# Routing and gathering from the unnormalised residual stream, with identity matmuls inside the first expert blocks, in a one-core encoder layer

## What is computed

```python
def rms_norm(x, g):
    y = x * lax.rsqrt(jnp.mean(x * x, axis=-1, keepdims=True) + EPS)
    return y * g

# h is the residual stream after cross attention; t = rms_norm(h, norm_ffn_g)
logits = jnp.dot(t, w_router) + b_router
top_v, top_i = lax.top_k(logits, TOP_K)
gates = jax.nn.softmax(top_v, axis=-1)
# for each expert e, for the tokens xb routed to it
hid = xb @ w_e1[e] + b_e1[e]
gate = jnp.minimum(hid[:, :D_FF], 7.0)
lin = jnp.clip(hid[:, D_FF:], -7.0, 7.0)
act = gate * jax.nn.sigmoid(1.702 * gate) * (lin + 1.0)
y = act @ w_e2[e] + b_e2[e]
# h + sum over the token's experts of gate weight * y, then rms_norm(., norm_final_g)
```

## Time and profile before

| | us |
|---|---|
| median of 3 runs (lowest, highest) | 1327.13 (1324.11, 1329.89) |
| the profiled execution | 1328.03 |
| its span, first to last instruction | 1326.1 |
| PE busy in the span | 1261.2 (95%) |
| DVE / ACT / POOL busy | 366.1 / 208.2 / 112.9 |
| PE waiting for weight chunks (L875: ring 15.0, stage 6.6, low 5.0) | 26.6 |
| moved by DMA | 456.83 MB, mean 344 GB/s |

### The profile page before, as it was taken

The page is one execution under the profiler, slowest core; times in us unless marked ns, Lnnn a source line. Parts: engine busy times, 40 slices in busy tenths (PEclk is TensorE's granted clock), DMA queues, the critical chain, the costliest instruction groups (busy, mean ns, idle before and its releaser), DMA issues.

```text
span 1326.1 us, 15280 instructions
## 1 busy us (share of the span) xinstructions
PE 1261.2 (95%) x6167; PEld 570.1 (43%) x6167; DVE 366.1 (28%) x785; ACT 208.2 (16%) x323; POOL 112.9 (9%) x109
## 2 busy tenths in 40 slices
PE   8999899999889999999999999999999999999996
PEld 3478785868643333333333333333333323333332
DVE  6478582021123111221112111122111111221112
ACT  2031422100311111111111111111111111111111
POOL 4599200010010000000000000000000000000000
PEclk9999899999999999999999999999999999999999
DMA  8533653449845999999999999999999999999995
GB/s 244 169 127 128 141 98 128 159 133 381 322 180 242 410 427 428 427 428 428 427 427 428 429 429 428 428 427 429 429 429 428 427 428 429 428 428 428 428 427 212
DMA packets 55128, 456.83 MB, mean 344 GB/s; under 512 B 4760, under 2 KB 6880, under 8 KB 30512
## 3 DMA queue, kind: packets, MB, share of 16 engines
q1 hardware_dynamic: 51744, 449.74, 82.3%
q0 software_dynamic: 2192, 5.99, 2.8%
q10 hardware_dynamic: 1152, 0.52, 0.2%
HBM read 454.11 MB, written 1.61 MB: 344 GB/s over the span
## 4 chain that ended last, share of the span: by engine, by line
PE 62%; DMA 29%; DVE 5%; ACT 3%; issue 1%; SPq 0%; ACTq 0%; DVEq 0%
PE pt L875 17%; DMA ring<-in_w_e 16%; PE pt L915 12%; DMA stage<-in_w_e 6%; DMA low<-in_w_e 6%; PE pt L476 6%; PE pt L489 6%; PE pt L524 4%; PE pt L456 3%; PE pt L842 3%; PE pt L829 3%; PE pt L537 2%; PE pt L881 1%; ACT wi_ L953 1%; DMA stage<-in_w_in 1%
## 5 line engine op out<-in xcount | busy, mean ns | idle before, releaser
L875 PE MATMUL pt<-ring,hres 128*64 128x512 f32 x1216 | 273.1, 595 | 15.3 <-DMA ring<-in_w_e 15.0
L875 PEld LDWEIGHTS pt<-ring,hres 128*64 128x64 f32 x1216 | 84.0, 137 | 198.7 <-issue 167.0
L915 PE MATMUL pt<-ring,wi_ 128*64 128x512 f32 x640 | 141.7, 595 | 5.4 <-ACT wi_ L953 5.4
L1560 DVE TENSOR_SCALAR hnt<-pt 128x512 f32<-128x512 f32 x32 | 22.1, 692 | 308.1 <-PE pt L875 308.1
L1506 DVE COPY ct_<-ct_ 128x2 f32 (+1 forms) x33 | 5.6, 170 | 363.7 <-PE pt L875 359.2
L875 PE MATMUL pt<-stage,hres 128*64 128x512 f32 x416 | 93.9, 595 | 6.6 <-DMA stage<-in_w_e 6.6
L875 PE MATMUL pt<-low,hres 128*64 128x512 f32 x416 | 93.8, 595 | 5.0 <-DMA low<-in_w_e 5.0
L1122 ACT ACTIVATE hnt<-hnt 128x512 f32<-128x512 f32 x32 | 20.2, 630 | 477.9 <-DVE hnt L1560 477.9
L915 PEld LDWEIGHTS pt<-ring,wi_ 128*64 128x64 f32 x640 | 44.5, 137 | 89.7 <-issue 82.4
L842 PE MATMUL pt<-big,lamb 64*128 64x512 f32 x256 | 63.6, 615 | 0.7 <-ACT big L953 0.7
L829 PE MATMUL pt<-a,ct_ 128*64 128x512 f32 x264 | 62.3, 593 | 0.0
(11 more groups left out here) (312 smaller groups left out, 1272.2 us busy)
## 6 DMA issues: line engine op xcount, KB each, us to landing
ring<-in_w_e SPq DMA_DIRECT2D x116, 2048.0 KB, 40.2
low<-in_w_e SPq DMA_DIRECT2D x38, 2048.0 KB, 41.0
stage<-in_w_e SPq DMA_DIRECT2D x38, 2048.0 KB, 40.1
stage<-in_w_in SPq DMA_DIRECT2D x16, 1024.0 KB, 6.7
stage<-in_w_xkv SPq DMA_DIRECT2D x8, 1024.0 KB, 5.9
stage<-in_w_mix_out SPq DMA_DIRECT2D x4, 1024.0 KB, 4.9
stage<-in_w_xq SPq DMA_DIRECT2D x4, 1024.0 KB, 4.9
stage<-in_w_xo SPq DMA_DIRECT2D x4, 1024.0 KB, 16.2
```

The lines of the kernel that those rows point to most:

```text
L875: last = pe.matmul(pt[PC][SLOTS * g:SLOTS * (g + 1), 512 * b:512 * (b + 1)], xT[:, k % 4, k // 4], ring_slot[n][:, c:c + 512], start=(k == ...
L915: last = pe.matmul(pt[PD][SLOTS * h:SLOTS * (h + 1), 512:1024], hT[:, c, g], ring_slot[n][:, D * c + 512 * h:D * c + 512 * (h + 1)], start ...
L1560: dve.tensor_scalar(hg, pt[PC][:, 0:512], GATE_MAX, None, ALU.min).then_inc(m_g2, 1)
```

## The change

- The router no longer reads normalised tokens. PE transposes the raw residual stream, in strided pieces (`by_k`), inside the second tile of `xo`: eight transposes for tile 0 after 4 matmuls, four for the first half of tile 1 after 12, the last four after `route(0)`. The second tile's residual sum is made in two halves.
- The gain is folded on POOL into the router weights, once, long before. The norm factor `r3` multiplies the logits (inside the bias addition) and the selection matrix `sel`. The gather reads `h3`, and the gain is applied in the product that replaces the copy to `xT` (`block_tokens`). `normed`, `gained_tile` and POOL's two products for this norm go away, and so does the load of the broadcast gain.
- The rank of expert 0 is used directly for its selection; positions, negated maxima, softmax of the gates, table of extra blocks and transposed gates come later, partly between the w_e1 chunks of the first block (`first_block_between`). The first gather is in two halves with copies on ACT and DVE.
- The identity matmuls: tile 0's two are around the rank matmuls, tile 1's go into blocks 0 and 1, `add_bias` into block 2. The bias matmuls of a block move from its first to its second w_e1 chunk.
- In every block ACT takes the sigmoid from PSUM without waiting for DVE's clamp, and the elementwise chain has three DVE operations where it had four.

The diff, cut to its core and with eight blanks of indentation taken off:

```diff
...
+xgn = a2[:, 0:512]
+xT_flat = a2[:, 512:1024]
 xT = xT_flat.rearrange("p (c n s) -> p c n s", c=4, n=2)
-hg, hl, hgl, hsg = (hnt[:, 512 * i:512 * (i + 1)] for i in range(4))
+hl, hsg, ysb = (hnt[:, 512 * i:512 * (i + 1)] for i in range(3))
+h0T = hnT[:, :, 0:P]
+h1T = a2[:, 0:KD * P].rearrange("p (k l) -> p k l", k=KD)
+by_k = [h3[:, t].rearrange("p (j q r) -> p j r q", j=W1_CHUNKS, r=2) for t in range(NT)]
+ffn_gain = gains[:, 3 * KD:4 * KD]
...
-    pool.dma_start(gffn, T["norm_ffn_g"].broadcast_to([P, D])).then_inc(s_gf, 16)
...
-    pool.wait_ge(s_gf, 16)
-    pool.wait_ge(S["tokp"], 8)
...
-        pool.tensor_tensor(xk, xk, gk, ALU.mult).then_inc(S["hn3"], 1)
+    pool.wait_ge(s_rt, 112)
+    pool.wait_ge(s_par, 112)
+    pool.tensor_tensor(wr, wr, ffn_gain.unsqueeze(2).to_broadcast([P, KD, NE]), ALU.mult).then_inc(S["wrg"], 1)
+    pool.wait_ge(S["wrg"], 1)
+    pool.tensor_scalar(be1[2 * NE:4 * NE, :], be1[2 * NE:4 * NE, :], 1.0, None, ALU.add).then_inc(S["wrg"], 1)
...
+    def turn_first():
+        pe.wait_ge(S["xh"], 1)
+        take(PA, ("hta", 1))
         for k in range(KD):
...
+            last = turn(pt[PA][:, P * k:P * (k + 1)], by_k[0][:, k // 2, k % 2])
+        last.then_inc(S["htp"], 1)
+    def turn_second(half):
+        pe.wait_ge(S["xh"], 2 + half)
+        if half == 0:
+            take(PC, ("hta", 2), ("htb", 1))
+        for k in range(4 * half, 4 * half + 4):
+            last = turn(pt[PC][:, P * k:P * (k + 1)], by_k[1][:, k // 2, k % 2])
+        last.then_inc(S["htp"], 1)
+    natural_tile(ws, 0, PC, hnT, ("xh", 1))
+    natural_tile(ws, 1, PD, hnT, ("xh", 3), inside={(0, 4): turn_first, (1, 4): lambda: turn_second(0)})
...
+        for k in range(k0, k1):
+            last = pe.matmul(pt[PB][:, 512 * t:512 * t + NE], (h0T, h1T)[t][:, k, :], wr[:, k, :],
                              start=(k == 0), stop=(k == KD - 1))
...
+        if k1 == KD:
+            last.then_inc(S["lgp"], 1)
+    def start_output(t, n):
+        return pe.matmul(pt[(PA, PB)[t]][:, 512 * n:512 * (n + 1)], ident, h3[:, t, 512 * n:512 * (n + 1)],
+                         start=True, stop=False)
...
+    ranks = pt[PB][:, 64:64 + NT * NE]
     pe.wait_ge(s_rt, 112)
...
-    route(0)
-    start_output(0)
-    turn_tile(xn, 1, PC, 3)
-    route(1)
-    pe.wait_ge(S["msk"], NT)
...
+    pe.wait_ge(S["wrg"], 2)
+    pe.wait_ge(S["hta"], 1)
+    take(PB)
+    route(0, 0, KD)
+    turn_second(1)
+    pe.wait_ge(S["hta"], 2)
+    route(1, 0, 4)
+    pe.wait_ge(S["htb"], 1)
+    route(1, 4, KD)
+    pe.wait_ge(S["msk"], 1)
+    pe.matmul(ranks[:, 0:NE], up, msk[:, 0, :], start=True, stop=True)
+    pe.matmul(ranks[:, NE:2 * NE], ones, msk[:, 0, :], start=True, stop=False)
+    take(PA)
+    start_output(0, 0)
+    pe.wait_ge(S["msk"], 2)
+    pe.matmul(ranks[:, NE:2 * NE], up, msk[:, 1, :], start=False, stop=True).then_inc(S["rkp"], 1)
     for t in range(NT):
...
-    start_output(1)
...
+        last = pe.matmul(pt[PB][0:NE, 576:577], msk[:, t, :], ones[:, 0:1], start=(t == 0), stop=(t == NT - 1))
+    last.then_inc(S["rkc"], 1)
+    start_output(0, 1)
...
+    take(PD)
     pe.wait_ge(m_sel, 1)
-    gather()
...
-    turn_block()
-    pe.wait_ge(S["cuv"], 1)
...
+    for j in range(2):
+        for t in range(NT):
+            for n in range(2):
+                last = pe.matmul(pt[PD][SLOTS * n:SLOTS * (n + 1), 512 * j:512 * j + 256], sel[:, t, :],
+                                 h3[:, t, 512 * n + 256 * j:512 * n + 256 * (j + 1)], start=(t == 0), stop=(t == NT - 1))
+        last.then_inc((S["xg0"], m_x)[j], 1)
+    for j in range(2):
+        pe.wait_ge((S["xga"], m_xn)[j], 1)
+        for c in range(2):
+            last = turn(pt[PD][:, 512 * j + P * c:512 * j + P * (c + 1)], xgn_by_c[:, j, c])
+        last.then_inc((S["xta0"], m_xt)[j], 1)
...
+    def first_block_between(j):
+        if j == 0:
+            pe.wait_ge(S["rkv"], 1)
+            pe.matmul(pt[PB][0:NE, 577:578], con[0:NE, C_TRI:C_TRI + NE], nbx[:, 0:1], start=True, stop=True).then_inc(S["cup"], 1)
+        elif j == 1:
+            pe.wait_ge(S["cuv"], 1)
+            pe.matmul(pt[PB][:, 640:640 + 2 * EXTRA + 1], ones[0:NE, :], blk[:, :], start=True, stop=True).then_inc(S["ovp"], 1)
+        elif j == 2:
+            pe.wait_ge(S["ovi"], 1)
+            pe.wait_ge(S["gdv"], NT)
+            for t in range(NT):
+                last = turn(pt[PB][0:NE, 768 + P * t:768 + P * (t + 1)], gate[:, t, :])
+            last.then_inc(S["gdp"], 1)
+    def block_of(it, q, r, early=None):
+        if early == 0:
+            pe.wait_ge(S["xT0"], 1)
+        else:
+            pe.wait_ge(m_xT, it + 1)
         for j in range(W1_CHUNKS):
...
+            if early == 0 and j == 1:
+                pe.wait_ge(m_xT, 1)
+            if j == 1:
+                for b in range(2):
+                    for g in range(2):
+                        i = NE * (2 * b + g)
+                        pe.matmul(pt[PC][SLOTS * g:SLOTS * (g + 1), 512 * b:512 * (b + 1)], ecol[i:i + NE, :],
+                                  be1[i:i + NE, :], start=False, stop=False)
             for k in (2 * j, 2 * j + 1):
                 for b in range(2):
                     for g in range(2):
                         c = 2048 * (k % 2) + D * b + 512 * g
                         last = pe.matmul(pt[PC][SLOTS * g:SLOTS * (g + 1), 512 * b:512 * (b + 1)], xT[:, k % 4, k // 4],
                                          ring_slot[n][:, c:c + 512], start=(k == 0), stop=(k == KD - 1))
...
             last.then_inc(m_w1u, 1)
+            if early == 0:
+                first_block_between(j)
...
-        if first:
-            add_bias().then_inc(m_sc, 1)
+        if early == 0:
+            start_output(1, 0).then_inc(m_sc, 1)
...
+            if early == 1:
+                pe.wait_ge(S["gda"], 1)
+                start_output(1, 1)
             pe.wait_ge(m_gs, it)
+            if early == 2:
+                add_bias()
             scatter(False).then_inc(m_sc, 1)
...
+    act.wait_ge(S["htp"], 3)
+    copy(h1T[:, 4:8], pt[PC][:, 512:1024].rearrange("p (k l) -> p k l", k=4)).then_inc(S["htb"], 1)
+    act.activation(st[:, 62:63], st[:, 60:61], ACT.Exp)
+    act.wait_ge(S["xg0"], 1)
+    copy(xgn[:, 0:256], pt[PD][:, 0:256]).then_inc(S["xga"], 1)
     for t in range(NT):
...
+        act.wait_ge(S["nmx"], t + 1)
+        act.activation(gate[:, t, :], lg[:, t, :], ACT.Exp, bias=nmax[:, t:t + 1]).then_inc(S["lex"], 1)
+    act.activation(st[:, 63:64], st[:, 60:61], ACT.Sigmoid)
...
-        act.wait_ge(m_g2, it + 1)
-        act.activation(hsg, hg, ACT.Sigmoid, scale=GATE_ALPHA).then_inc(m_sig, 1)
...
-    norm_tile(3, 0)
-    gained_tile(3, 0, PA)
-    residual_tile(1, PD, "xh")
-    norm_tile(3, 1)
...
+    dve.tensor_copy(ecol, con[:, C_M32:C_M32 + 1].to_broadcast([P, SLOTS]))
+    r3 = st[:, 14:14 + NT]
...
+    dve.wait_ge(S["htp"], 1)
+    dve.tensor_copy(h0T, pt[PA][:, :].rearrange("p (k l) -> p k l", k=KD)).then_inc(S["hta"], 1)
+    dve.wait_ge(S["root"], 6)
+    link(dve.reciprocal(r3[:, 0:1], r3[:, 0:1]))
+    slab_done(dve, "xo0")
+    dve.tensor_tensor(h3[:, 1, 0:512], h3[:, 1, 0:512], pt[PD][:, 0:512], ALU.add).then_inc(S["xh"], 1)
+    dve.wait_ge(S["htp"], 2)
+    dve.tensor_copy(h1T[:, 0:4], pt[PC][:, 0:512].rearrange("p (k l) -> p k l", k=4)).then_inc(S["hta"], 1)
+    slab_done(dve, "xo1")
+    dve.tensor_tensor(h3[:, 1, 512:1024], h3[:, 1, 512:1024], pt[PD][:, 512:1024], ALU.add).then_inc(S["xh"], 1)
     def top(t):
         dve.wait_ge(S["lgp"], t + 1)
...
+        link(dve.scalar_tensor_tensor(lg[:, t], pt[PB][:, 512 * t:512 * t + NE], r3[:, t:t + 1], brt, ALU.mult, ALU.add))
         link(dve.max(top8[:, t], lg[:, t]))
...
+        dve.tensor_copy(nmax[:, t:t + 1], top8[:, t, 0:1])
...
+    def slots_of_tokens():
+        for t in range(NT):
+            last = dve.tensor_scalar(sel[:, t], io, pse[:, 0, t:t + 1], r3[:, t:t + 1], ALU.is_equal, ALU.mult)
...
+    dve.wait_ge(S["rkp"], 1)
+    link(dve.scalar_tensor_tensor(pse[:, 0, :], ranks[:, :, 0], 1.0, msk[:, :, 0], ALU.add, ALU.mult))
+    slots_of_tokens().then_inc(m_sel, 1)
+    for t in range(NT):
...
+    link(dve.scalar_tensor_tensor(posn, ranks, 1.0, msk, ALU.add, ALU.mult))
+    dve.wait_ge(S["rkc"], 1)
...
+    g3 = ffn_gain.rearrange("p (n c) -> p c n", c=4).unsqueeze(3)
+    def block_tokens(lo, hi, at=0):
+        src = pt[PD][:, at + P * lo:at + P * hi].rearrange("p (c n s) -> p c n s", n=2, s=SLOTS)
+        return dve.tensor_tensor(xT[:, lo:hi], src, g3[:, lo:hi].to_broadcast([P, hi - lo, 2, SLOTS]), ALU.mult)
     dve.wait_ge(m_x, 1)
-    dve.tensor_copy(xgn, pt[PD][:, 0:512]).then_inc(m_xn, 1)
+    dve.tensor_copy(xgn[:, 256:512], pt[PD][:, 512:768]).then_inc(m_xn, 1)
+    dve.wait_ge(S["xta0"], 1)
+    block_tokens(0, 2).then_inc(S["xT0"], 1)
+    dve.wait_ge(m_xt, 1)
+    block_tokens(2, 4, 256).then_inc(m_xT, 1)
+    for t in range(NT):
...
+    dve.wait_ge(S["gdv"], NT)
```

(10 more changed lines are left out.)

147 lines of the change are left out of this document (47 added, 100 removed).

## The result

The changed kernel takes 1318.93 us, median of six runs (1317.42 to 1322.68), the kernel before 1328.47 on the same chip (six runs, 1324.11 to 1329.89). The ratio is **0.9936 [0.9916, 0.9955]**, 9.5 us less. Six more runs of the same changed kernel, beside 23 of the kernel before, gave 1318.20 and 1328.10, 0.9926 [0.9910, 0.9942]. The forecast was 1317.0 with a range of 1313.5 to 1320.5.

A forecast was written before the change was run, and what follows sets the result against it. The stream of weights (DMA), unable to start before the router stage, was taken as the bound. 9.2 + 1.0 + 0.3 = 10.5 us off the profiled 1328.03 gives 1317.5, by the median 1316.6; forecast 1317.0, range 1313.5 to 1320.5.

The forecast's parts named there:

- The bound: Late blocks: the stream of weights sets the end, so the router stage before it counts microsecond for microsecond.
- Inside `xo`: Second tile of xo: twelve transposes where eight were add 0.44 us; strided reads of h3 taken at nothing.
- The 9.2 us of the stage: Router stage: first expert matmul at 397.9 instead of 407.08, 9.2 us sooner.
- clock rival: Router stage: the clock falls to half inside the new stretch, costing 1.3 to 3.4 us, 1318.3 to 1320.4; chance 0.30.
- The 1.0 us of the bias matmuls: First chunk: four bias matmuls (1.02) go behind it, which frees it 1.0 us sooner.
- 0.3 less: First block: the DMA pause of 1.4 us before chunk 14 shrinks, a gain taken as 0.3 us.
- Blocks 1 and 2: They get 0.98 and 3.63 us more PE work, which the stream's lag uses up: zero, at most 0.5 lost.
- Signs that the prediction set itself: Profile after: logits end near 391.6, first expert matmul 397 to 399, chunk 10 issued 401 to 403, at most one pause.
- At nothing: Parts priced at zero: shorter DVE chain, earlier sigmoid, POOL's work, the missing gain load, the tail after the last w_e1 chunk.
- The first block did not stall: Rival: in the first block PE waits for cuv, ovi and gdv, losing 2 to 7 us, 1319 to 1324; chance 0.07.
- hidden anyway: Rival: the stream does not depend on PE at the start, so nothing moves, 1328; chance 0.03.
- PE-bound: Rival: strided transposes and broadcast product lengthen blocks until PE is the bound; 1.7 us per block gives 1335 and above; chance 0.02.

The follow-up runs named there:

- wide_logits: Changed kernel with router logit matmuls 128 columns wide instead of 32, the extra columns unused: 1316.52 us, ratio 0.9925 to the kernel before.
- wait_before_stream: Changed kernel with five more identity matmuls, results thrown away, ahead of the first expert matmul: 1324.39 us, ratio 0.9975 to the kernel before.
- bias_first: Changed kernel with the four bias matmuls back in every block's first weight chunk: 1317.46 us, ratio 0.9925 to the kernel before.
- identity_out: Changed kernel with tile 0's two identity matmuls moved into blocks 0 and 1 and add_bias to block 4: 1317.87 us, ratio 0.9915.
- identity_split: Changed kernel with half an identity matmul at each of two stage places, one in block 0, two in block 1, bias in block 4: 1317.63 us, ratio 0.9923.
- after_again: The changed kernel itself run once more, unaltered: 1318.20 us, ratio 0.9926 to the kernel before.
- chain_alone: Kernel before with only the new elementwise chain (sigmoid, three DVE operations, POOL's addition to be1): 1328.25 us, ratio 1.0001.
- table_first: Changed kernel with the table of extra blocks and the gate transposes before the first block again: 1323.16 us, ratio 0.9960 to the kernel before.
- identity_between: Changed kernel with tile 0's two identity matmuls moved ahead of tile 1's logits: 1321.26 us, ratio 0.9940 to the kernel before.
- work_in_blocks: Changed kernel with one more identity matmul, result thrown away, in each of blocks 5 to 31: 1321.82 us, ratio 0.9949 to the kernel before.

## Why the prediction was right, and where terms were off

**The bound.** Right. The last 500 us are DMA's, and the router stage counts at least one for one: 4.35 us added there cost 6.2, and 4.3 added ahead of chunk 14 cost 5.7, while 23.5 us of work in the blocks cost 3.6.

**Inside `xo`.** +0.44 forecast, +0.54 found. The strided reads cost 0.1 at most; they were taken at nothing.

**The 9.2 us of the stage.** This is the term that was mis-sized most. The forecast had 10.5 from `xo`'s end to the first expert matmul (387.4 to 397.9); it took 13.04, so that the piece gave 7.10 - 0.54 = 6.6. The working was sound: where the clock held, the same code needed 9.9, and 10.17 with wide logits. What came is the **clock rival**, above the middle of its price: 13.04 - 10.17 = 2.9, within its 1.3 to 3.4. It had a chance of 0.30 and should have had more: a half clock after transposes and 32-column logits was in the profile of before, and what spoke against the rival, that the waits were gone, did not matter. PE was busy for all of 384 to 392, and the clock fell within it. The rule of the Trainium skill, "TensorE: Matmul & The Clock Gate", Part 4 (PE-mode transpose), that transposes do not count as PE work in the same way, pointed at the right stretch. No run here shows that it is the cause: *wide_logits* and *wait_before_stream* have the same transposes and 1.00 in 384 to 392. The cause of the fall stays open.

**The 1.0 us of the bias matmuls.** Wrong as a gain of its own. The move freed chunk 10 by 1.17, and the profile of *bias_first* shows it worth nothing. The step that failed is the first one, "the end is therefore the time of chunk 10's issue, plus 180 chunks, plus any pause": it is true as a sum, but the pause before chunk 14 and chunk 10's issue are not independent. Chunk 14's issue is the later of the two gates, and what chunk 10 gains is handed back in the pause. In the 60 us after chunk 10's issue DMA moved 407 GB/s before and 404 after, which against 428 is 2.9 and 3.4 us of missing bytes. So the pause grew by about 0.5, where 0.3 less was forecast.

**Blocks 1 and 2, "zero, at most 0.5 lost".** Mis-sized: 1.0 us is lost in front of chunk 26, in both profiles of the changed kernel. The forecast let the lead of the stream pay for the identity matmul and for `add_bias` at the full clock. In the profile the clock is at 0.57 in 472 to 476, over the scatter behind `add_bias`. Without that fall (*bias_first*), or with `add_bias` in block 4 (*identity_out*, *identity_split*), nothing is lost there.

**The same sum by the right measure.** `xo`'s end to chunk 14 went from 45.85 to 36.94: 8.4 less with `xo`'s 0.54, against 10.5 forecast. Had the clock held, as in *wide_logits*, it would be 34.07, 11.2 less with `xo`. The second pause takes 1.0 off either. By the medians, the parts of it are: the table and the gates behind the first chunks 5.0, the norm factor off the path 3.7 to 4.4 (they overlap through the clock), the identity matmuls 0 to 1 more if they leave the stage (and 3 lost if they stand between the logits), the bias matmuls and the elementwise chain nothing that can be told.

**Signs that the prediction set itself.** Its times are on the scale of the profile of before, 4.7 later than this one. On that scale the second tile's logits end at 391.5 (forecast 391.6), the first expert matmul starts at 400.5 (forecast 397.9, and "later than 400" was to show it wrong), and chunk 10 goes out at 404.2 (forecast 401.7). Two pauses follow, not one. So the median came out 1.9 above the forecast although the pieces gave 7.4 instead of 10.5. That closeness is in part luck: the total also holds losses of the kernel before that the forecast did not speak of.

**Why the medians still differ by 9.5 to 9.9.** A part goes with the clock over the whole run. The 23 runs of the kernel before that stood beside *after_again* follow it, but for one (1326.4 at 0.993): 1323.8 to 1324.4 at 0.993 and 0.994, 1325.7 and 1326.3 at 0.991, 1327.9 to 1330.4 at 0.988 and 0.989, where fifteen of them lie. The changed kernel gave 1315.6 at 0.994, 1318.2 to 1320.0 at 0.991 and 1322.7 at 0.989. At equal clock that is 8.2 to 8.8, about 7 and, from one run, about 6; the rest is that the kernel before mostly ran at 0.989 and the changed one at 0.991. The two profiles of the old front show where it loses: ahead of `xo` (4.5, the profile of before) or in the stage and the first block (4.6, *chain_alone*). Both have nearly the same span. How often each came, and why, was not traced.

**At nothing.** The chain (1.0001), blocks 1 and 2, POOL and the tail were stepped at nothing. The chain is shown, blocks 1 and 2 are told above. The tail's +1.73 is the last w_e1 chunk at a lower clock (5.35 for 3.65), which also stands in *table_first*, *identity_between* and *wide_logits*, and not in *after_again* or *bias_first*.

**The other rivals.** The first block did not stall for `cuv`, `ovi` or `gdv`, hidden anyway fell with *wait_before_stream*, and PE-bound with *work_in_blocks*.

## What to carry to other kernels

Where a stream of weights sets the end, don't stop at the first chunk that waits for a buffer: follow the queue to the last one that still waits for PE in the warm-up, for work moved from before the first gate to between the two only moves the pause. Then look at the blocks behind it, into which the work was put off: here 1.0 us of it came back as a pause in the third. Work that the stream waits for is worth its full time at any distance from the end, and the cheapest way to find it is to defer what only later blocks need (here the table and the gates, 5.0 us). Before a stretch is tightened, look at the granted clock in it in several profiles, not one: here it decided 2.9 us.

## What the runs showed of the hardware

- PE busy for 4.00 of 4.00 does not keep the clock. In 384 to 388 transposes, logits of 32 columns and rank matmuls filled it, and the clock was at 0.50 in 388 to 392. The same code up to the gather kept 1.00 in another execution (*wait_before_stream*).
- The sixteen matmul records of a tile's logits take 1.87 with 32 columns and 1.95 with 128.
- The device time follows the mean granted clock from run to run, by 0.8 to 1 us per 0.001 in the kernel before and, over twelve runs, by 1.2 to 1.4 in the changed one, although DMA bounds the late part; the falls that the traces show before chunk 14's issue, in the third block and in the tail are where it can count.
- The stream varies: from chunk 14's issue to the last w_e1 chunk it took 867.0 to 870.5 us in fourteen profiles. Up to 3.0 us of a profile's stream is the pause in front of chunk 26, the rest is not explained. A single profile can't show a gain of 2 us in this kernel.
- With 27 added matmuls PE stood still for 3.25 us before the last scatter without any visible wait, in the one trace taken. It is not explained.
